# A hand-scheduled transformer pair on one Trainium2 core: the output norm of the token mixing moved behind the next round's substitution

## What is computed

```python
xs = tuple(jnp.moveaxis(t, 1, 0) for t in (r4, k4, v4, kk, a4, w4))
_, ys = lax.scan(step, jnp.zeros((B, H, N, N), f32), xs)      # S = S*w + sa (kk a)^T + v k^T ; y = S r
y = jnp.moveaxis(ys, 0, 1)
mean = jnp.mean(y, axis=-1, keepdims=True)
var = jnp.mean(jnp.square(y - mean), axis=-1, keepdims=True)
y = ((y - mean) * lax.rsqrt(var + RW_GN_EPS)).reshape(B, T, RW_WIDTH)
y = y * ln_x_w.astype(f32) + ln_x_b.astype(f32)
bonus = jnp.sum(r4 * k4 * r_k.astype(f32), axis=-1, keepdims=True) * v4
y = (y + bonus.reshape(B, T, RW_WIDTH)) * g.astype(f32)
...
y_a = _rwkv7_time_mix(...) @ w_branch_rwkv[l]
y_b = _dsa_attention(...) @ w_branch_dsa[l]
h = h + (g_a * y_a + g_b * y_b) @ w_out[l]
```

## Time and profile before

| | us |
|---|---|
| median of three runs | 3675.16 |
| lowest, highest | 3669.25, 3679.57 |
| the profiled execution's time | 3677.76 |
| its span in the trace | 3675.6 |
| PE busy in the span | 3555.4 (97%) |
| DVE, ACT, POOL busy | 2151.6, 1752.4, 345.7 |
| mean granted TensorE clock | 0.982 of full |

### The profile page before, as it was taken

The page is one execution under the profiler, slowest core; times in us unless marked ns, Lnnn a source line. Parts: engine busy times, 40 slices in busy tenths (PEclk is TensorE's granted clock), DMA queues, the critical chain, the costliest instruction groups (busy, mean ns, idle before and its releaser), DMA issues. The chain is left out here.

```text
span 3675.6 us, 50843 instructions
## 1 busy us (share of the span) xinstructions
PE 3555.4 (97%) x20474; PEld 3019.7 (82%) x20474; DVE 2151.6 (59%) x2871; ACT 1752.4 (48%) x2601; POOL 345.7 (9%) x217
## 2 busy tenths in 40 slices
PE   8899999989989999999999999999999999999999
PEld 7777777678779999888899998887788877788777
DVE  4676556545565578655544455555688875555454
ACT  5454333324434478544444444444655554444763
POOL 0000000000049900000000000000022210000000
PEclk9999999899999999999999999999999999999999
DMA  6454334345535555555555565655433335455334
GB/s 223 157 181 146 103 136 141 136 173 200 216 117 183 183 174 172 183 216 184 193 206 186 213 253 187 225 188 189 174 137 141 134 133 189 171 190 192 128 138 160
DMA packets 112138, 638.53 MB, mean 174 GB/s; under 512 B 18698, under 2 KB 24618, under 8 KB 40152
## 3 DMA queue, kind: packets, MB, share of 16 engines
q1 hardware_dynamic: 106664, 622.98, 47.6%
q0 software_dynamic: 5296, 13.15, 1.1%
HBM read 611.10 MB, written 21.54 MB: 172 GB/s over the span
## 5 line engine op out<-in xcount | busy, mean ns | idle before, releaser
L222 DVE TENSOR_TENSOR lo_w<-ring,hi_w 128x1024 fp32r<-128x1024 f32 x500 | 612.5, 1225 | 983.8 <-ACT hi_w L216 975.5
L216 ACT CAST hi_w<-ring 128x1024 fp32r<-128x1024 f32 x540 | 568.9, 1054 | 949.5 <-DMA ring<-in_wstream 925.7
L224 DVE TENSOR_TENSOR lo_w<-ring,hi_w 128x1024 fp32r<-128x1024 f32 x500 | 612.2, 1224 | 0.0
L1996 PE MATMUL PS<-hi_x,hi_w 128*128 128x256 f32 x2048 | 581.1, 284 | 4.9 <-POOL lo_w L224 2.7
L1996 PE MATMUL PS<-hi_x,lo_w 128*128 128x256 f32 x2048 | 575.1, 281 | 0.0
L1996 PE MATMUL PS<-lo_x,hi_w 128*128 128x256 f32 x2048 | 570.9, 279 | 0.0
L217 ACT CAST hi_w<-ring 128x1024 fp32r<-128x1024 f32 x540 | 564.8, 1046 | 0.0
L2022 PE MATMUL PS<-hi_w,hi_g 128*128 128x512 f32 x1024 | 404.0, 395 | 1.1 <-issue 1.1
L2022 PE MATMUL PS<-lo_w,hi_g 128*128 128x512 f32 x1024 | 403.5, 394 | 0.0
L2022 PE MATMUL PS<-hi_w,lo_g 128*128 128x512 f32 x1024 | 403.2, 394 | 0.0
L1996 PEld LDWEIGHTS PS<-hi_x,hi_w 128*128 128x128 f32 x2048 | 385.5, 188 | 5.4 <-ACT GG L2204 3.1
(11 more groups left out here) (581 smaller groups left out, 5786.2 us busy)
## 6 DMA issues: line engine op xcount, KB each, us to landing
ring<-in_wstream SPq DMA_DIRECT2D x540, 1024.0 KB, 4.8
other_G<-staged SPq DMA_DIRECT2D x32, 256.0 KB, 6.0
hot<-other_G SPq DMA_DIRECT2D x8, 1024.0 KB, 6.8
gates_dram<-gst POOLq DMA_DIRECT2D x8, 512.0 KB, 4.6
x_dram<-x SPq DMA_DIRECT2D x2, 2048.0 KB, 12.2
x<-x_dram SPq DMA_DIRECT2D x2, 2048.0 KB, 9.5
prev<-RKV POOLq DMA_DIRECT2D x6, 508.0 KB, 5.3
x<-in_x SPq DMA_DIRECT2D x4, 512.0 KB, 6.5
```

The costliest lines, as they stand in the source:

```text
L216: a.copy(hi_w[s][:, 0:HALF], ring[s][:, 0:HALF]).then_inc(S(f"hi{s}"), 1)
L222: v.tensor_tensor(lo_w[s][:, 0:HALF], ring[s][:, 0:HALF], hi_w[s][:, 0:HALF].bitcast(F32), ALU.subtract)
L224: v.tensor_tensor(lo_w[s][:, HALF:UNIT], ring[s][:, HALF:UNIT], hi_w[s][:, HALF:UNIT].bitcast(F32), ALU.subtract)\
L1996: m = nc.tensor.matmul(PS[:, s, 0:T], wa[s][:, k * P:(k + 1) * P], xa[:, k, :], start=(k == 0 and p == 0), stop=(k == KC - 1 and p == 2))
```

## The change

On VectorE `center` of the rounds 0 to 2 goes from offset 15.75 to 19 and `finish` from 16.25 to 19.75; on ScalarE the root goes from 16 to 19.25. As the next round's `solve` ends at 12 + 6.5 = 18.5, the norm of round n now stands behind it and not in front of it. For round 2 this puts `finish` at unit 79.0, inside the branch projection, so `turn_y(2)` and both `turned_y(2)` go from unit 77 to unit 80. `turn_y(3)` on TensorE goes one quarter later within unit 85, from quarter 1 to quarter 2; its `turned_y(3)` stay. SP's `lines(1)` goes from unit 66 to unit 68. The offsets of round 3's norm stay. TensorE's `gates_up` stays.

```diff
                 if u == 66:
                     gups(1)
+                if u == 68:
                     lines(1)
...
-                    if (u, g) == (WIN + 9, 1):
+                    if (u, g) == (WIN + 9, 2):
                         turn_y(3)
...
-                    if u == WIN + 1 and g < 3:
+                    if u == WIN + 1 and g < 2:
                         turn_y(g)
+                    if (u, g) == (WIN + 4, 2):
+                        turn_y(2)
                     quarter(u, g)
...
-                    for n in late_due(U, g, 16, 13):
+                    for n in late_due(U, g, 19.25, 13):
                         a.wait_ge(S("gn_var"), n + 1)
...
-                    if U == WIN + 1 and g:
+                    if U == WIN + 1 and g in (1, 2):
                         turned_y(g - 1)
+                    if (U, g) == (WIN + 4, 3):
+                        turned_y(2)
...
-                    for n in late_due(U, g, 15.75, 12.75):
+                    for n in late_due(U, g, 19, 12.75):
                         center(n)
-                    for n in late_due(U, g, 16.25, 13.25):
+                    for n in late_due(U, g, 19.75, 13.25):
                         finish(n)
...
-                    if U == WIN + 1 and g:
+                    if U == WIN + 1 and g in (1, 2):
                         turned_y(g - 1)
+                    if (U, g) == (WIN + 4, 3):
+                        turned_y(2)
```

## The result

The changed kernel takes 3690.74 us (median of 9 runs, 3686.09 to 3701.02) against 3676.09 us for the kernel before in the same comparison: a ratio of 1.0041, with a 95% interval of 1.0032 to 1.0049. It is slower by 14.7 us. The forecast was 3693, in the range 3682 to 3703.

The account below looks back on a forecast made before the run. TensorE's matmul stream plus its stands, where VectorE is late, bounds the kernel. Two rounds at 8.3 + 0.9 = 9.2 us give 18.4; less 0.7 in round 3, +17.7 on 3675.2 makes 3692.9, rounded to 3693; range 3682 to 3703.

Parts of the forecast that it names:

- The half in front of the substitution: VectorE before the substitution, rounds 1 and 2: without the norm it idles some 8 us and starts the substitution 0.2 us earlier.
- The half behind: VectorE from the substitution to `spread`, rounds 1 and 2: the moved norm makes `spread` 8.25 us later.
- ScalarE's queue: Conversion and gate tile behind the root: VectorE waits 1.2 us, TensorE stands 4.1 us for the gate, at no additional cost.
- The clock term: TensorE after its new stands, rounds 1 and 2: extra half-clock stretch costs 0.9 us a round, ends 0 and 2.
- Round 3: Units 76 to 83: `gated` 3.5 us earlier, then given back; net -0.7 us, from -3.5 to +2.
- `turn_y(3)`: Unit 85, one quarter later on TensorE, inside the wait for y_done: 0, from -0.2 to +1.2 us.
- SP's `lines(1)`: SP's wait for y_done, behind unit 68's transfer: 0, any late transfer covered by TensorE's stand.
- The two rivals that held the sign open: No change: 8.4 us find room behind the substitution, about 3673 (0.13). Faster: the stands go, 18.4 us, 3657 (0.05).

Follow-up runs that it names:

- e5_finish_only: The changed kernel with `center` and ScalarE's root of rounds 0 to 2 back in front of the substitution, only `finish` behind; 3678.20 us, ratio 1.001 to the kernel before.
- e6_keys_later: The kernel before with `keys_norm` of every round moved behind the previous round's `spread`, where VectorE idles; 3670.58 us, ratio 0.9982.
- e4_root_later: The changed kernel with ScalarE's root and VectorE's `finish` of rounds 0 to 2 at offset 20.75, `center` still at 19; 3696.79 us, ratio 1.0047 to the kernel before.
- e1_turn3_back: The changed kernel with only `turn_y(3)` back at quarter 1 of unit 85; 3692.89 us, ratio 1.0041 to the kernel before.
- e3_third_only: The changed kernel with the norms of rounds 0 and 1 back in front and `turn_y(3)` back at quarter 1; 3676.34 us, ratio 1.000 to the kernel before.

## Why the prediction was right

*The half in front of the substitution is free.* Right: forecast 8 us of idle time and a start 0.2 us earlier; measured 8.16 us in both rounds, with a start 0.3 us earlier in round 1 and 0.1 us later in round 2.

*The half behind is on the path, 8.25 us on `spread`.* Right: 7.96 and 7.97 us in the two rounds. The step could be halved (e5_finish_only: 3.5 for a forecast 3.4) and turned round (in round 1 e6_keys_later has 2.3 us less between the substitution and `spread`, and L851's stand shrinks by 2.3; in round 2 both shrink by 0.7). That VectorE's work and not the queue on ScalarE sets the end was argued in the forecast; e4_root_later showed it, by removing the queue and leaving 10 us before L852.

*ScalarE's queue.* Right in kind: the new wait is 1.24 us (1.2), TensorE's stands for the gate tile 3.33 and 3.76 us (4.1), covered by the wait for `spread`. Whether it was covered to nothing is open: with it gone, e4_root_later's two rounds are 2.3 and 1.6 us shorter, of which 1.08 are the high part's wait, and the rest is within the spread.

*The clock term, 0.9 us a round.* Not settled. By the first pair of profiles the stretches rose 7.6 and 7.8 us for 8.0 us of later `spread`, which makes it -0.4 and -0.2 us; by the means of all profiles with these rounds 8.5 and 9.5, which makes it +0.5 and +1.5. The forecast's 0.9, its lower end 0 and nearly its upper end 2 all lie in that. What is shown is that slow matmuls in front of a stand only shorten it. The rounds of e1_turn3_back are those of the changed kernel. After the stand for the gate tile in round 1 some six of its matmuls ran at half clock, in the changed kernel some fourteen; L852 then stood 6.31 us instead of 4.85, and the stretch is 126.35 us against 126.07:

```profile
445.24:571.59 126.35, 115.72 (x787) 88.68 (x787) 68.41 (x110) 45.68 (x60) 6.44 (x11) 0.93 0.36 124
```

That is also why L852's stands, forecast at 5 to 8 us, were 4.85 and 4.94 in the changed kernel. L852 of round 3, forecast 16 to 18 us later, came about 14 us later, counted from unit 50.

*Round 3, -0.7 us.* Right within a microsecond: +0.1 us in the changed kernel, -0.9 in e1_turn3_back, and -1.0 alone. The substitution started 2.8 us earlier (forecast 2.7), the first `gated` came 3.3 us earlier (3.5), the stand was 6.27 us (6.1), `spread` 1.3 us earlier. It was given back behind: 1.6 us before `turn_y(2)`, which the forecast had not named, and in the changed kernel slow matmuls after L868 that before did not have.

*`turn_y(3)`, 0 with a top of 1.2 us.* The step that failed: +2.1 us, shown by e1_turn3_back. The forecast said itself that the moved quarter had filled just the time in which `turned_y(3)` is made, and priced the gap it leaves at no waiting. The quarter shortened the first stand by 1.4 us (5.05 to 3.66) and left a second of 2.42, so 1.0 us more of standing. The top of 1.2 us, six slow matmuls more, is what happened beside it: twelve instead of six, 1.1 us.

*SP's `lines(1)`, 0.* TensorE waits for no transfer that it did not wait for before, and e3_third_only, which has it at unit 68, takes the time of before; its y_done is early there, so the late wait was not tried by itself.

The terms add to 17.6 us by the first pair of profiles and to 19.4 by the means, against 17.7 in the forecast, and the runs give 14.7 (11.8 to 18.0). The path and the size of its main term were forecast from the rows and came so. That the median came within 3 us of 3693 is partly luck: with `turn_y(3)` at its 2.1 us the forecast's own sum is 19.8 us, above what the runs allow. The two rivals that held the sign open fell at the place named for them: VectorE has 1.4 us and not 8 behind the substitution.

## What to carry to other kernels

Work that fills an engine's wait is free, and a busy engine doesn't show which of its work that is: ask of each stretch what it would do if the work were gone, wait for someone else, or run on. Moving work "off the front" of a critical result puts it behind, where the same result is awaited; here the move that paid was of other work, from between the result and its consumer into an idle stretch. It gave 4 us in the medians (7 by the ratio) by itself, and 16 to 18 once the consumer was no longer queued behind a conversion that waits for a transfer. Look at what a late wait holds up in its own queue as well: the root of eight numbers in each partition held ScalarE for 9.6 us, and with it a conversion for 8.5 us and a gate tile for about 5.

## What the runs showed of the hardware

Filling a wait can cost more than it saves, if the work filled another wait where it stood. The quarter before `turn_y(3)`, 1.4 us of matmuls at full clock, was worth 2.1 us in its old place. With 3.66 us, a transpose, and 2.42 us of standing, about twelve matmuls of 512 columns ran at half clock in each of the three kernels that have this pattern and the old place of `keys_norm`; with the single stand of 5.05 us about six, in each of the four that have that one.

A stand's length alone does not tell its slow clock. In unit 56 the changed kernel had about fourteen slow matmuls after a stand of 3.33 us, e1_turn3_back about six after 3.52 us at the same place. And with the same stands of 3.61 us, the matmuls of units 62 to 74 took 115.1 us in the profile of before and 112.0 in e3_third_only. A stand that ends a run of slow matmuls hides their cost: it was shorter by about what they took longer (L852 4.85 against 6.31 us).
